# Hybrid decoder trunk: three adding transfers per up slab, and another order for forming slabs

## The chip, the cores and the metric

The kernel runs on one core of a Trainium2 chip (trn2). The metric is device time in microseconds (us), the median of repeated executions. Engines are named as in the profile: PE (TensorE, matrix products), ACT (ScalarE), DVE (VectorE), POOL (GpSimd), SP (SyncE, which here only issues DMAs). Each engine runs its own instructions in order; engines wait for one another by semaphores.

## The reference, cut to what matters

All of it is float32, with 16 meta tokens ahead of 512 tokens and a model width of 1024, in two layers:

```
u = rms_norm(h, norm_mix[l]);  proj = u @ w_in[l]          # conv branch, q, k, v, gates
...                                                        # depthwise conv, differential attention
h = h + merged @ w_o[l]
u = rms_norm(h, norm_mlp[l])
h = h + jnp.square(jax.nn.relu(u @ w_up[l])) @ w_down[l]   # w_up 1024 x 4096, w_down 4096 x 1024
```

The change touches only how the product `u @ w_up[l]` is fed.

## The kernel before

**Weights.** All weights come in slabs of 128 partitions x 2048 float32 (1 MB). There are two buffers of each kind, used in turn (`b = m % 2`): `w_raw` takes what SP loads, and a number is split into a high part (`w_hi`, rounded to fp32r) and a low part (`w_lo`, the rest). Each product of matrices is three matmuls: high by high, high by low, low by high.

**The MLP.** Per layer there are four groups g; each has four up slabs m = 0 to 3 and then four down slabs. An up slab is multiplied by a seven-product scheme on quarters of the matrix (`PRODUCTS`, in the order p1, p5, p2, p6, p7, p4, p3; 12 matmuls each). A slab has quarters A11, A21, A12, A22 of `QUAD` columns. Products p1, p5, p2 and p6 use the early forms (A11; the sum S1; A12; the sum S2), in `w_hi` and `w_lo`. Products p7, p4 and p3 use the late forms (S3, A22, S4), in `x_hi` and `x_lo`. Below, "slab 0 to 3" is an up slab m of a group.

**Who forms what.**
- DVE `sums_early(g, m)` (L1960, L1961) makes S1 and S2 from the landed slab; `sums_late(g, m)` (L1972, L1973) makes the two late sums, once `x_lo` of the slab before is finished.
- ACT `early_neg(g, m)` (L1224, L1225) writes the negated early forms from `w_raw` and `s2` into `w_lo`; `early_high` (L1230, L1231) writes the rounded ones into `w_hi`; `late_plain` (L1238) and `late_sums` (L1244) write `x_hi`.
- POOL `early_low(g, m)` issues two adding DMAs (L735 of 768 KB and L736 of 256 KB). These are written by the source as `w_lo += w_raw` and `w_lo += s2`, and both count on one semaphore `low_landed[b]`. They follow a small instruction `tick` (L734), which waits for `w_neg`.
- POOL `late_parts(g, m, parts)` (L747) computes `x_lo` in three parts of four instructions each: part 0 (plain, A22), part 1 (first late sum) and part 2 (second late sum).
- ACT `first_product` (L1252) copies p1's result out of PSUM, and `hidden_high(m, j)` (L1258 relu, L1259 square) handles one half of a finished slab. DVE `u2_sum`, `c22_sum`, `c21_sum`, `c12_sum` (L2008 to L2027) add up the seven products; `hidden_low` (L2038) and `square_up` (L2033) finish the hidden values.

**What sets the order.** The order on each engine is written out by hand in the loops over g and m. The waits that matter here are these:
- PE starts p1 of slab m when both transfers of its low part have landed, `early_high(m)` is done, and DVE has done `u2_sum(m - 1)`. PE starts p5 after `c22_sum(m - 1)`, p6 after `first_product(m)`, p7 after part 1 of `x_lo(m)`, and p3 after part 2.
- DVE `sums_early(3)` stands in the pass m = 1, between `c22_sum(1)` and `c21_sum(1)`.
- ACT `early_neg(3)` stands in the pass m = 1, ahead of `late_sums(2)` and `hidden_high(1, 1)`.
- POOL has, in every group, part 0 of `x_lo(2)`, then `early_low(3)`, then parts 1 and 2 of `x_lo(2)`, then all of `x_lo(3)`, then the low part of the first down slab (L634).
- SP loads the slab m + 2 (L604) when the low part of slab m has landed, among other waits.

Of the kernel before, what the change touches and what calls it, by code (L numbers as in the profile page):

```python
# [26 lines left out]
ALU = mybir.AluOpType  # L27
# [252 lines left out]
def build(nc, x_t, w_slabs, pvecs, rows_in, ident_in, mask_in, identb_in, out, h_spill, r_rows):  # L280
    ctx = ExitStack()
    with ctx:
# [161 lines left out]
        u_raw, t_raw, f_hi, f_ready = sem("u_raw"), sem("t_raw"), sem("f_hi"), sem("f_ready")  # L444
        sum_early, sum_late, sums_read = sem("sum_early"), sem("sum_late"), sem("sums_read")
        w_neg, w_form, w_late = sem("w_neg"), sem("w_form"), sem("w_late")
        low_landed, late_low = [sem("low_landed0"), sem("low_landed1")], sem("late_low")
        q_full, p1_done, u2_done, c22_done, tile_sum, relu_done = (sem(x) for x in ("q_full", "p1_done", "u2_done", "c22_done", "tile_sum", "relu_done"))
        v_chain, a_chain, p_chain = sem("v_chain"), sem("a_chain"), sem("p_chain")

# [28 lines left out]
        def a_read(layer, tile, k):  # L479

            return k + ((layer * A_TILES + tile) // 2 + 1)
# [88 lines left out]
        @block.sync  # L570
        def _(sp):
            slabs = w_slabs.rearrange("(i b) p c -> b i p c", b=2)
            for k, landed in enumerate(h_landed):
                if k in (1, 2):
                    half = slice((k - 1) * SLAB // 2, k * SLAB // 2)
                    sp.dma_start(w_raw[:, 0, half], slabs[0, 0, :, half]).then_inc(w_landed[0] if k == 2 else half_landed, 16)
                sp.dma_start(h[:, 2 * k:2 * k + 2, :], x_t[:, 2 * k:2 * k + 2, :]).then_inc(landed, 16)
            for dst, src in ((ident, ident_in), (maskb, mask_in), (identb, identb_in)):
                sp.dma_start(dst[:], src).then_inc(in_landed, 16)
            sp.dma_start(w_raw[:, 1, :], slabs[1, 0]).then_inc(w_landed[1], 16)  # L580

            def load_slabs(first, last):

                with sp.Fori(first // 2, last // 2) as i:
                    for b in range(2):
                        sp.wait_ge(w_ready, 2 * i + (b - 1))
                        sp.dma_start(w_raw[:, b, :], slabs[b, ds(i, 1)].rearrange("o p c -> p (o c)")).then_inc(w_landed[b], 16)

            start = 2
            for layer in range(LAYERS):  # L590
                load_slabs(start, up_slab(layer, 0, 2))
                for g in range(4):
                    for m in range(8):
                        s = up_slab(layer, g, m + 2)
                        if m < 4:
                            n = up_nth(layer, g, m)
                            sp.wait_ge(low_landed[n % 2], 32 * (n // 2 + 1))
                            sp.wait_ge(w_form, n + 1)
                            sp.wait_ge(late_low, 2 * n + 1)
                            sp.wait_ge(sum_late, n + 1)  # L600
                        else:
                            sp.wait_ge(w_ready, s - 1)
                        if s < LAYERS * SLABS:
                            sp.dma_start(w_raw[:, s % 2, :], slabs[s % 2, s // 2]).then_inc(w_landed[s % 2], 16)  # L604
                start = (layer + 1) * SLABS + 2
            for i in range(NT):

                sp.wait_ge(h_new, (LAYERS - 1) * NT + i + 1)
                sp.dma_start(out[:, i, :], h[:, i, META:T]).then_inc(stored, 16)
            sp.wait_ge(stored, 16 * NT)  # L610
# [3 lines left out]
        def _(pool):  # L614
# [73 lines left out]
            for layer in range(LAYERS):  # L688
# [39 lines left out]
                def early_low(g, m):  # L728

                    b, n = m % 2, up_nth(layer, g, m)  # L730
                    pool.wait_ge(w_neg, n + 1)
                    if n > 1:
                        pool.wait_ge(low_landed[b], 32 * (n // 2))
                    chain.link(nc.gpsimd.tensor_tensor(tick[:], ones[:, 0:1], ones[:, 0:1], ALU.mult))  # L734
                    pool.dma_start(w_lo[:, b, 0:3 * QUAD], w_raw[:, b, 0:3 * QUAD], accum_op=ALU.add).then_inc(low_landed[b], 16)  # L735
                    pool.dma_start(w_lo[:, b, 3 * QUAD:SLAB], s2[:, b, :], accum_op=ALU.add).then_inc(low_landed[b], 16)  # L736

                def late_parts(g, m, parts):

# [10 lines left out]
                plain, summed = (0,), (1, 2)  # L750
                early_low(0, 0)
                for g in range(4):
                    early_low(g, 1)
                    if g == 0:
                        late_parts(g, 0, plain + summed)
                        late_parts(g, 1, plain + summed)
                        early_low(g, 2)
                    else:
                        late_parts(g, 1, plain)
                        early_low(g, 2)  # L760
                        late_parts(g, 1, summed)
                    late_parts(g, 2, plain)
                    early_low(g, 3)
                    late_parts(g, 2, summed)
                    late_parts(g, 3, plain + summed)
                    for d in range(4):
                        down_low(g, d)
                    if g < 3:
                        early_low(g + 1, 0)
                        late_parts(g + 1, 0, plain + summed)  # L770
# [4 lines left out]
        def _(pe):  # L775
# [70 lines left out]
            def up_products(layer, g, m):  # L846
# [2 lines left out]
                n2 = span(layer)[1] // 2  # L849
                formed = layer * N_FORMS if (g, m) == (0, 0) else None  # L850
                tiles = (layer * A_TILES + A_MLP + 8 * g) // 2
                pe.wait_ge(low_landed[b], 32 * (n // 2 + 1))
                pe.wait_ge(w_form, n + 1)
                if n:
                    pe.wait_ge(u2_done, n)
                if formed is not None:
                    pe.wait_ge(f_ready, formed + 2 * KH)
                for k, (f, x, name) in enumerate(PRODUCTS):
                    if name == "p5" and n:
                        pe.wait_ge(c22_done, n)  # L860
                    if name == "p6":
                        pe.wait_ge(p1_done, n + 1)
                    elif name == "p2" and m < 2:
                        if (g, m) == (0, 1):
                            pe.wait_ge(sums_read, layer + 1)
                        pe.wait_ge(a_free[0], tiles)
                        pe.wait_ge(a_free[1], tiles)
                    elif name == "p2":
                        pe.wait_ge(hid_ready, 2 * (n - 1))
                    elif name == "p7":  # L870
                        if m:
                            pe.wait_ge(hid_ready, 2 * n - 1)
                        pe.wait_ge(late_low, 2 * n + 2)
                    elif name == "p3":
                        pe.wait_ge(w_ready, s + 1)
# [287 lines left out]
        def _(act):  # L1163
# [250 lines left out]
            for layer in range(LAYERS):  # L1414
# [91 lines left out]
                for i in range(NT):  # L1506
                    if i in (1, 3):
                        w_high_part(layer, s0 + 6 + i // 2)
                    if i == NT - 3:
                        early_neg(layer, 0, 0)  # L1510
                    if i == NT - 1:
                        early_neg(layer, 0, 1)
                    act.wait_ge(a_free[i % 2], a_read(layer, A_O, i // 2))
                    norm_raw(layer, i)
                    form_plain(layer, i)
                    if i == NT - 1:
                        late_plain(layer, 0, 0)
                    form_sum(layer, i)
                    if i == NT - 1:
                        first_product(layer, 0, 0)  # L1520
                        late_sums(layer, 0, 0)
                    if i >= KH:
                        form_last(layer, i)
                    norm_square(layer, i)
                    if i == NT - 2:
                        early_high(layer, 0, 0)
                    if i == NT - 1:
                        early_high(layer, 0, 1)
                for kk, (what, g) in enumerate(MLP_ORDER):
                    if what == "up":  # L1530
                        for m in range(4):
# [5 lines left out]
                                first_product(layer, g, m)  # L1537
                            if m == 1 and g == 0:
                                late_sums(layer, g, 1)
                            if m:  # L1540
                                hidden_high(layer, g, m - 1, 0)
                            if m == 1 and g == 0:
                                early_neg(layer, g, 2)
                            if m < 3:
                                late_plain(layer, g, m + 1)
                            if m < 3 and (m or g):
                                early_high(layer, g, m + 1)
                            if m == 1 or m == 0 and g:
                                early_neg(layer, g, m + 2)
                            if m < 3 and (m or g):  # L1550
                                late_sums(layer, g, m + 1)
                            hidden_high(layer, g, m, 1)
# [26 lines left out]
        def _(dve):  # L1579
# [176 lines left out]
            for layer in range(LAYERS):  # L1756
# [291 lines left out]
                for kk, (what, g) in enumerate(MLP_ORDER):  # L2048
                    if what == "up":
                        for m in range(4):  # L2050
                            if m:
# [3 lines left out]
                                    announce(dve, V.tensor_scalar(halves(r_inv2, layer), mlp_sum(layer)[1], 1.0 / D, NORM_EPS, ALU.mult, ALU.add), sums_read, layer + 1)  # L2055
                                hidden_low(g, m - 1, 1)
                                square_up(g, m - 1, 0)
                            if m == 1 and g == 0:
                                sums_early(g, 2)
                            if m < 3 and (m or g):  # L2060
                                sums_late(g, m + 1)
                            if m:
# [8 lines left out]
                            square_up(g, m, 1)  # L2071
                            if m == 0 and g == 0:
                                sums_late(g, 1)
                        c12_sum(g, 3)
                        hidden_low(g, 3, 1)
                        square_up(g, 3, 0)
# [100 lines left out]
```

## Time and profile before

| | |
|---|---|
| device time, 3 runs | median 1875.01 us (1873.65 to 1876.04) |
| profiled execution | 1878.18 us, of which the span is 1876.4 us |
| busy share of the span | PE 96%, PEld 88%, DVE 70%, POOL 63%, ACT 44% |
| chain that ended last | PE 69%, POOL 10%, DVE 7%, DMA 5%, ACT 4%, issue 4% |
| up slabs (matmuls of L883) | 578 to 632 us and 678 to 907 us in layer 0, 1502 to 1556 us and 1601 to 1827 us in layer 1, with down slabs between |

The profile is that of one execution. Busy time of PE is the time in which matmuls were in flight. The chain is followed back from the last instruction to what released each wait, so it names the work that set the end. A wait's releaser is the one whose signal came last.

### The profile page before, as it was taken

The numbers are of one execution on the slowest core, as the hardware profiler recorded it, in microseconds if no ns is written. First come the engines' busy times: TensorE is split into PE (matmuls) and PEld (weight loads), VectorE is DVE, ScalarE is ACT, GpSimd is POOL, SyncE is SP. The second block draws the span as 40 slices with busy tenths as digits, with TensorE's granted clock in tenths as the row PEclk, the third lists the DMA queues.
The fourth block names the chain that finished last, engine by engine and source line by source line (L and its number), as shares of the span: only waits on it lengthen the run. The fifth ranks groups of instructions, "written<-read, shape, count | busy, mean of one in ns | idle before, by whom it ended". The sixth has DMA issues, their size and how long they took to land.

```text
span 1876.4 us, 34787 instructions
## 1 busy us (share of the span) xinstructions
PE 1806.8 (96%) x13053; PEld 1650.9 (88%) x13053; DVE 1311.5 (70%) x2085; ACT 823.4 (44%) x1745; POOL 1173.1 (63%) x2240
## 2 busy tenths in 40 slices
PE   9999999999997999999999999999999989999989
PEld 8999888889997999999999998887678788888787
DVE  7998888777456555646569989888865664647462
ACT  4135565436246343535421355553453563525260
POOL 4777445546774666666687664446477566676664
PEclk9999999999998999999999999999999989999999
DMA  4222111112325463637432221111233362736362
GB/s 176 90 91 68 30 62 46 64 50 92 137 90 137 132 159 113 166 104 173 135 113 90 88 71 46 46 49 65 67 108 126 106 151 99 178 107 164 116 159 85
DMA packets 34794, 194.54 MB, mean 104 GB/s; under 512 B 4048, under 2 KB 4432, under 8 KB 16992
## 3 DMA queue, kind: packets, MB, share of 16 engines
q1 hardware_dynamic: 21888, 147.01, 22.9%
q0 software_dynamic: 9216, 33.56, 9.6%
q10 hardware_dynamic: 3552, 12.15, 1.8%
q8 instruction: 84, 1.38, 0.3%
q14 instruction: 54, 0.44, 0.1%
HBM read 154.85 MB, written 4.29 MB: 85 GB/s over the span
## 4 chain that ended last, share of the span: by engine, by line
PE 69%; POOL 10%; DVE 7%; DMA 5%; ACT 4%; issue 4%; DVEq 0%; POOLq 0%; ACTq 0%
PE psum L789 40%; PE psum L928 13%; PE psum L883 4%; POOL w_lo L634 3%; DMA w_lo<-s 3%; POOL w_lo L627 3%; PE psum L1025 2%; PE psum L993 2%; DMA w_raw<-w_slabs 2%; PE psum L942 2%; POOL x_lo L747 2%; PE psum L1013 1%; ACT e L1343 1%; DVE h L2103 1%; PE psum L1070 1%
## 5 line engine op out<-in xcount | busy, mean ns | idle before, releaser
L634 POOL TENSOR_TENSOR w_lo<-w_raw,w_hi 128x128 fp32r<-128x128 f32 x1152 | 560.6, 525 | 222.5 <-ACT w_hi L1325 194.3
L789 PE MATMUL psum<-u,w_hi 128*128 128x264 f32 (+1 forms) x2112 | 407.7, 308 | 9.1 <-POOL w_lo L627 5.0
L789 PEld LDWEIGHTS psum<-u,w_hi 128*128 128x128 f32 x2112 | 310.0, 189 | 31.5 <-POOL w_lo L627 6.5
L789 PE MATMUL psum<-hid,w_hi 128*128 128x264 f32 (+1 forms) x1536 | 328.3, 322 | 5.7 <-POOL w_lo L634 5.7
L560 DVE SCALAR_TENSOR_TENSOR psum<-xg,pvec,psum 128x512 f32<-128x512 f32 x440 | 301.0, 750 | 4.6 <-DVE xg L1815 2.2
L928 PE MATMUL psum<-w_hi,u 128*128 128x256 f32 x1536 | 287.7, 287 | 0.1
L789 PEld LDWEIGHTS psum<-hid,w_hi 128*128 128x128 f32 x1536 | 237.3, 188 | 30.3 <-issue 7.0
L789 PE MATMUL psum<-u,w_lo 128*128 128x264 f32 (+1 forms) x1056 | 251.2, 304 | 0.0
L928 PEld LDWEIGHTS psum<-w_hi,u 128*128 128x128 f32 x1536 | 237.6, 189 | 10.7 <-issue 10.3
L627 POOL TENSOR_TENSOR w_lo<-w_raw,w_hi 128x128 fp32r<-128x128 f32 x480 | 237.4, 532 | 2.5
L928 PE MATMUL psum<-w_lo,u 128*128 128x256 f32 x768 | 215.9, 281 | 0.0
L1325 ACT CAST w_hi<-w_raw 128x2048 fp32r<-128x2048 f32 x72 | 137.4, 1908 | 173.8 <-PE psum L789 173.8
L789 PE MATMUL psum<-hid,w_lo 128*128 128x264 f32 (+1 forms) x768 | 204.8, 321 | 0.0
L883 PE MATMUL psum<-uh,w_hi 128*128 128x264 f32 (+1 forms) x512 | 152.6, 298 | 36.6 <-DMA w_lo<-s 15.8
L789 PEld LDWEIGHTS psum<-u,w_lo 128*128 128x128 f32 x1056 | 170.6, 189 | 8.5
L2102 DVE TENSOR_TENSOR down_tmp<-psum,r_inv 128x512 f32<-128x512 f32 (+1 forms) x56 | 39.1, 699 | 165.9 <-PE psum L789 165.7
L883 PE MATMUL psum<-ul,w_hi 128*128 128x264 f32 (+1 forms) x512 | 148.4, 290 | 0.0
L883 PE MATMUL psum<-uh,w_lo 128*128 128x264 f32 (+1 forms) x512 | 148.1, 289 | 0.0
L928 PEld LDWEIGHTS psum<-w_lo,u 128*128 128x128 f32 x768 | 145.4, 189 | 0.0
L747 POOL TENSOR_TENSOR x_lo<-s,x_hi 128x128 fp32r<-128x128 f32 x256 | 127.7, 906 | 22.7 <-ACT x_hi L1244 22.7
L883 PEld LDWEIGHTS psum<-uh,w_hi 128*128 128x128 f32 x512 | 100.4, 196 | 42.6 <-DMA w_lo<-s 17.8
L789 PEld LDWEIGHTS psum<-hid,w_lo 128*128 128x128 f32 x768 | 127.7, 188 | 11.2
(253 smaller groups left out, 3606.6 us busy)
## 6 DMA issues: line engine op xcount, KB each, us to landing
w_raw<-w_slabs SPq DMA_DIRECT2D x135, 1024.0 KB, 4.9
w_lo<-w_raw POOLq DMA_DIRECT2D x32, 768.0 KB, 5.9
w_lo<-s POOLq DMA_DIRECT2D x32, 256.0 KB, 6.8
h<-x_t SPq DMA_DIRECT2D x4, 528.0 KB, 7.3
h<-x_t ACTq DMA_DIRECT2D x1, 2112.0 KB, 9.5
h_spill<-h ACTq DMA_DIRECT2D x8, 264.0 KB, 2.7
h<-h_spill ACTq DMA_DIRECT2D x1, 2112.0 KB, 8.4
out<-h SPq DMA_DIRECT2D x8, 256.0 KB, 2.2
```

Source lines behind the costliest of these rows:

```text
L560: return nc.vector.scalar_tensor_tensor(out=done if ends else acc, in0=x, scalar=w, in1=done if begins else acc, op0=ALU.mult, op1=ALU.add)
L627: last = nc.gpsimd.tensor_tensor(w_lo[:, b, c:c + P], w_raw[:, b, c:c + P], w_hi[:, b, c:c + P], ALU.subtract)
L634: last = nc.gpsimd.tensor_tensor(w_lo[:, b, c:c + P], w_raw[:, b, c:c + P], w_hi[:, b, c:c + P], ALU.subtract)
L747: last = nc.gpsimd.tensor_tensor(x_lo[:, b, cut], source[:, c:c + P], x_hi[:, b, cut], ALU.subtract)
L789: last = nc.tensor.matmul(psum[:, 2 * slot + j, 0:n], w[:, b, cut], src[:, part, kc, at0:at0 + n], start=(kc == 0 and m == 0), stop=(kc == ...
L883: last = nc.tensor.matmul(quad(layer, m, name), w[:, cut], act_[:, x, kc, 0:n2], start=(kc == 0 and j == 0), stop=(kc == KH - 1 and j == 2))
L928: done = nc.tensor.matmul(psum[0:tn, B_BANK[n], 0:2 * P], u[:, part, kc, t0:t0 + tn], w[:, b, kc * 2 * P:(kc + 1) * 2 * P], start=k == 0, ...
L942: last = nc.tensor.matmul(psum[0:2 * META, bank, 0:2 * P], meta_u[:, kc, :], w[:, b, kc * 2 * P:(kc + 1) * 2 * P], start=kc == 0 and w is ...
L993: nc.tensor.matmul(psum[0:tn, banks[c], at0:at0 + k1 - k0], qk[rows64, 0, hh % 2, qp, t0:t0 + tn], qk[rows64, 1, hh % 2, kp, k0:k1], start ...
L1025: last = nc.tensor.matmul(psum[:, bank, (i - 1) * P:SEQ], v_sb[0:kn, hh // 2 % 2, j, cut], a_t[0:kn, b0:b0 + n, :].rearrange("p a b -> p ( ...
L1325: nc.scalar.copy(w_hi[:, b, :], w_raw[:, b, :]).then_inc(w_high, 1)
L2102: announce(dve, V.tensor_tensor(row(down_tmp[:], layer), a_ps(layer, j), row(r_inv2[:], layer), ALU.mult), a_free[j], a_read(layer, A_MLP ...
```

## The change

It does four things.

1. The low part of an up slab comes by three adding DMAs of 256, 512 and 256 KB in place of two of 768 and 256 KB. Each has its own semaphore. PE waits for the first ahead of p1, for the second ahead of p5 and for the third ahead of p6. SP and POOL wait for all three.
2. In the first group of each layer, slab 2 is formed earlier on DVE and ACT: `sums_early(0, 2)` moves to the end of the pass m = 0, and `early_neg(0, 2)` goes ahead of `hidden_high(0, 0)`. On POOL, part 0 of `x_lo(0)` goes ahead of `early_low(1)`, and `early_low(2)` goes ahead of part 2 of `x_lo(1)`.
3. In the last step of the output projection, `late_plain(0, 0)` goes to the front and `early_neg(0, 1)` behind the last `form_sum`.
4. In all eight groups `early_neg(3)` moves on ACT from the pass m = 1 to the pass m = 2, behind `first_product(2)`.

```diff
-        low_landed, late_low = [sem("low_landed0"), sem("low_landed1")], sem("late_low")
+        low_landed, late_low = [[sem(f"low_landed{b}{part}") for part in "abc"] for b in range(2)], sem("late_low")
...
-                    pool.dma_start(w_lo[:, b, 0:3 * QUAD], w_raw[:, b, 0:3 * QUAD], accum_op=ALU.add).then_inc(low_landed[b], 16)
-                    pool.dma_start(w_lo[:, b, 3 * QUAD:SLAB], s2[:, b, :], accum_op=ALU.add).then_inc(low_landed[b], 16)
+                    pool.dma_start(w_lo[:, b, 0:QUAD], w_raw[:, b, 0:QUAD], accum_op=ALU.add).then_inc(low_landed[b][0], 16)
+                    pool.dma_start(w_lo[:, b, QUAD:3 * QUAD], w_raw[:, b, QUAD:3 * QUAD], accum_op=ALU.add).then_inc(low_landed[b][1], 16)
+                    pool.dma_start(w_lo[:, b, 3 * QUAD:SLAB], s2[:, b, :], accum_op=ALU.add).then_inc(low_landed[b][2], 16)
...
                 for g in range(4):
+                    if g == 0:
+                        late_parts(g, 0, plain)
                     early_low(g, 1)
                     if g == 0:
-                        late_parts(g, 0, plain + summed)
-                        late_parts(g, 1, plain + summed)
+                        late_parts(g, 0, summed)
+                        late_parts(g, 1, plain + summed[0:1])
                         early_low(g, 2)
+                        late_parts(g, 1, summed[1:2])
...
-                pe.wait_ge(low_landed[b], 32 * (n // 2 + 1))
+                pe.wait_ge(low_landed[b][0], 16 * (n // 2 + 1))
...
-                    if name == "p5" and n:
-                        pe.wait_ge(c22_done, n)
+                    if name == "p5":
+                        pe.wait_ge(low_landed[b][1], 16 * (n // 2 + 1))
+                        if n:
+                            pe.wait_ge(c22_done, n)
                     if name == "p6":
+                        pe.wait_ge(low_landed[b][2], 16 * (n // 2 + 1))
                         pe.wait_ge(p1_done, n + 1)
...
                     if i == NT - 3:
                         early_neg(layer, 0, 0)
+                    act.wait_ge(a_free[i % 2], a_read(layer, A_O, i // 2))
+                    if i == NT - 1:
+                        late_plain(layer, 0, 0)
+                    norm_raw(layer, i)
+                    form_plain(layer, i)
+                    form_sum(layer, i)
                     if i == NT - 1:
                         early_neg(layer, 0, 1)
-                    act.wait_ge(a_free[i % 2], a_read(layer, A_O, i // 2))
-                    norm_raw(layer, i)
-                    form_plain(layer, i)
-                    if i == NT - 1:
-                        late_plain(layer, 0, 0)
-                    form_sum(layer, i)
...
                             if m == 1 and g == 0:
                                 late_sums(layer, g, 1)
+                                early_neg(layer, g, 2)
+                            if m == 2:
+                                early_neg(layer, g, 3)
                             if m:
                                 hidden_high(layer, g, m - 1, 0)
-                            if m == 1 and g == 0:
-                                early_neg(layer, g, 2)
                             if m < 3:
                                 late_plain(layer, g, m + 1)
                             if m < 3 and (m or g):
                                 early_high(layer, g, m + 1)
-                            if m == 1 or m == 0 and g:
-                                early_neg(layer, g, m + 2)
+                            if m == 0 and g:
+                                early_neg(layer, g, 2)
...
-                            if m == 1 and g == 0:
-                                sums_early(g, 2)
                             if m < 3 and (m or g):
                                 sums_late(g, m + 1)
...
                             square_up(g, m, 1)
                             if m == 0 and g == 0:
                                 sums_late(g, 1)
+                                sums_early(g, 2)
```

## Rows read from the trace of the kernel before

**Rows 1.** Waits of PE, whole span: us in total, times, longest us.
```profile
PE psum L883 <- DMA w_lo<-s: 15.8, 8, 5.5
```

**Rows 2.** Chain that ended last, layer 0 group 1: start us, us, what.
```profile
682.34 7.82 DMA w_lo<-s
...
690.20 7.60 PE psum L883 x60
...
698.76 0.70 DVE w_raw L1960
...
700.22 1.49 ACT w_lo L1224
...
702.79 0.87 POOL w_lo L735
...
704.56 3.39 POOL x_lo L747 x8
...
723.83 0.36 PE psum L789
```

**Rows 3.** The chain in other groups, same columns: layer 0 groups 2, 3; layer 1.
```profile
781.44 8.68 DMA w_raw<-w_slabs
...
873.55 3.38 POOL x_lo L747 x8
...
1792.31 10.19 DMA w_raw<-w_slabs
```

**Rows 4.** The chain in the first group of layer 0 and of layer 1.
```profile
608.67 22.96 PE psum L883 x168
...
1533.15 22.72 PE psum L883 x168
```

**Rows 5.** Timeline of ACT, layer 0 group 1: start us, us, engine, line.
```profile
703.06 0.60 ACT L1258 ACTIVATE relu<-psum 128x528 f32<-128x528 f32 x1
703.70 0.65 ACT L1259 ACTIVATE hid<-relu 128x528 fp32r<-128x528 f32 x1
704.25 0.36 ACT L1252 COPY r_inv<-psum 128x264 f32<-128x264 f32 x1
```

**Rows 6.** Timelines of DVE and of POOL, layer 0 group 1.
```profile
700.22 0.44 DVE L2022 TENSOR_TENSOR psum<-psum,q_u 128x264 f32<-128x264 f32 x1
...
703.38 1.19 POOL L736 DMA_DIRECT2D w_lo<-s  x1
703.94 4.00 POOL L747 TENSOR_TENSOR x_lo<-s,x_hi 128x128 fp32r<-128x128 f32 x8
```

**Rows 7.** Timeline of PE, layer 0 group 1: the first matmul of slab 2's p7.
```profile
706.43 0.36 PE L883 MATMUL psum<-uh,x_hi 128*128 128x264 f32 x1
```

**Rows 8.** SP's load of slab 3, layer 0 group 1; its time to landing (last).
```profile
690.17 0.33 SPq L604 DMA_DIRECT2D w_raw<-w_slabs  x1
...
w_raw<-w_slabs SPq DMA_DIRECT2D x1, 1024.0 KB, 7.6
```

**Rows 9.** Timelines of POOL and of DVE in the first group of layer 0.
```profile
595.96 4.36 POOL L747 TENSOR_TENSOR x_lo<-s,x_hi 128x128 fp32r<-128x128 f32 x8 [5.20 <-ACT x_hi L1244]
...
600.42 0.69 DVE L1972 TENSOR_TENSOR s<-w_raw,s 128x512 f32<-128x512 f32 x1 [1.69 <-POOL x_lo L747]
...
604.33 0.76 DVE L1960 TENSOR_TENSOR w_raw<-w_raw 128x512 f32<-128x512 f32 x1
```

**Rows 10.** Stretch in the first group: busy us (instructions) by engine, then PEclk.
```profile
607.00:614.00 7.00, 5.33 (x25) 5.33 (x26) 2.81 (x5) 5.31 (x10) 5.45 (x12) 0.51 0.79 178
```

**Rows 11.** The page's DMA queue (MB, share of 16 engines) and DMA issues (landing).
```profile
q0 software_dynamic: 9216, 33.56, 9.6%
...
w_lo<-w_raw POOLq DMA_DIRECT2D x32, 768.0 KB, 5.9
w_lo<-s POOLq DMA_DIRECT2D x32, 256.0 KB, 6.8
...
out<-h SPq DMA_DIRECT2D x8, 256.0 KB, 2.2
```

More of the change, by code:

```diff
@@ L596, in _ @@
                             n = up_nth(layer, g, m)
-                            sp.wait_ge(low_landed[n % 2], 32 * (n // 2 + 1))
+                            for landed in low_landed[n % 2]:
+                                sp.wait_ge(landed, 16 * (n // 2 + 1))
                             sp.wait_ge(w_form, n + 1)
@@ L732, in early_low @@
                     if n > 1:
-                        pool.wait_ge(low_landed[b], 32 * (n // 2))
+                        for landed in low_landed[b]:
+                            pool.wait_ge(landed, 16 * (n // 2))
                     chain.link(nc.gpsimd.tensor_tensor(tick[:], ones[:, 0:1], ones[:, 0:1], ALU.mult))
-                    pool.dma_start(w_lo[:, b, 0:3 * QUAD], w_raw[:, b, 0:3 * QUAD], accum_op=ALU.add).then_inc(low_landed[b], 16)
-                    pool.dma_start(w_lo[:, b, 3 * QUAD:SLAB], s2[:, b, :], accum_op=ALU.add).then_inc(low_landed[b], 16)
+                    pool.dma_start(w_lo[:, b, 0:QUAD], w_raw[:, b, 0:QUAD], accum_op=ALU.add).then_inc(low_landed[b][0], 16)
+                    pool.dma_start(w_lo[:, b, QUAD:3 * QUAD], w_raw[:, b, QUAD:3 * QUAD], accum_op=ALU.add).then_inc(low_landed[b][1], 16)
+                    pool.dma_start(w_lo[:, b, 3 * QUAD:SLAB], s2[:, b, :], accum_op=ALU.add).then_inc(low_landed[b][2], 16)
                 def late_parts(g, m, parts):
```

## The prediction

> **What bounds the kernel now.** I read the shares first: PE is busy for 96% of the span and holds 69% of the chain that ended last. So nearly everything is paced by PE, and only a wait of PE, or a chain that goes round PE through a group, can move the end. Second, I read PE's waits. The largest releaser is the low part of an up slab, 15.8 us in 8 waits [rows 1]. The change is aimed at these. Two of them are the first groups' slab 2, 5.4 and 5.5 us; the other six share 4.9 us.
>
> Third, I read the chain that ended last, in order of time, because a wait that goes is worth only what the next bound leaves. In layer 0's group 1 [rows 2] it runs: landing of slab 1's low part, PE to 697.8, DVE `sums_early(3)` at 698.76, ACT `early_neg(3)` at 700.22, POOL's DMAs at 702.79, `x_lo(2)` parts 1 and 2 at 704.56, then DVE, ACT and POOL until the first down slab starts at 723.83. So from `sums_early(3)` on, the group's end is not set by PE. It is set by one chain through `early_neg(3)` and `early_low(3)`, since POOL computes parts 1 and 2 of `x_lo(2)` only behind `early_low(3)`. In other groups the chain doesn't even enter by PE's wait: in layer 0's group 2 and layer 1's group 3 it goes from slab 1's low part through SP's load of slab 3 (8.68 and 10.19 us) to `sums_early(3)` [rows 3]. Layer 1's groups 1 and 2 look the same; layer 0's group 3 enters by `x_lo(1)` on POOL.
>
> **The six later groups.** Removed: the wait of p1(1) for the full low part, 4.9 us in all [rows 1]. The first 256 KB should be down about 3.3 us after issue. That is worked out from the queue's rate, 33.56 MB in 9.6% of 1876 us, or 186 GB/s, so 1.4 us for 256 KB and 4.2 us for 768 KB. The 768 KB landed in 5.9 us, which leaves 1.7 us around the data [rows 11]. That wait then ends before PE arrives, and the second and third parts have 1.45 and 4.4 us more (one and three products of 12 matmuls).
>
> Added on the chain, per group:
> - `early_neg(3)` stood directly behind `sums_early(3)`. Now `hidden_high(1, 1)` and `first_product(2)` go ahead of it on ACT, and `hidden_high(1, 1)` waits for `c21_sum(1)`, which stands behind `sums_early(3)` on DVE. That is 0.44 us for L2022 [rows 6], and relu, square and copy, from 703.06 to 704.61, 1.5 us [rows 5]: 1.9 us.
> - A third DMA ahead of `x_lo(2)` part 1. Two issues start 0.59 us apart and the next instruction 0.56 us later [rows 2, 6]: 0.6 us.
> - Sum 2.5 us. `early_neg(3)` also waits for slab 2's p1 to be finished, which is earlier than this in every group.
>
> This delay has no cover. Part 1 of `x_lo(2)` ended at half of its 4.00 us, 705.9 [rows 6], and p7(2) began at 706.43 [rows 7]. So PE will reach p7(2) and stand there 2 to 4 us. Behind it nothing in the group has slack, as rows 2 show up to 723.83.
>
> What comes off depends on how early `sums_early(3)` can start:
> - Layer 0, group 1: PE is 1.5 us earlier, but slab 3 lands at 690.17 + 7.6 = 697.8 [rows 8], against the start at 698.76. So 0.9 us comes off: +1.6.
> - The four groups bound by the load: the load still waits for all of the low part, whose bytes haven't changed. Nothing comes off, or up to 0.9 us if slab 3's packets get through sooner between smaller low ones. I take 0.3 off, nearer to none, as no row shows such a gain: 4 x 2.2 = +8.8.
> - Layer 0, group 3: `x_lo(1)` stands behind `early_low(2)` [rows 3] and gets a third DMA too: 2.5 + 0.6 = +3.1.
>
> Together +13.5 us, with bounds of +9 (0.9 off in all six, no extra DMA) and +16.
>
> **The first groups.** The 5.4 us before p1(2) is mostly removed: `sums_early(2)` needs no wait for `square_up(0, 0)` any more. But look at what ends later. A third DMA ahead of `x_lo(0)` part 1 makes PE 0.6 late. `x_lo(1)` parts 1 and 2 took 4.36 us from 595.96 [rows 9], 2.2 us each. Now part 1 ends at 598.7. Then `early_low(2)` takes 0.5 for the tick and its gap, and 3 x 0.57, and part 2 ends at 603.1, where it was 600.3. DVE's `sums_late(2)` waits for that. It began at 600.42 and DVE then ran without a pause to `sums_early(3)` at 604.33 [rows 9], so that now starts at 607.1 and ends at 608.7. The 1.9 us of before puts `early_neg(3)` at 610.6. In rows 2 it is 2.57 us from there to the first DMA, 613.2; then 1.7 for three DMAs and 2 x 2.1 for the parts, 619.1. In group 1, part 2 ended at 707.95 and the down slab started at 723.83, 15.9 us later [rows 2]: 635.0. Before, it started at 608.67 + 22.96 = 631.6 [rows 4]. So +3.4, and I take +3.3 for each layer, as layer 1's stretch has nearly the same length (22.72). Bounds: 0, if the chain behind part 2 shrinks by what PE gained, and +5.
>
> That contains the clock. After the 5.4 us pause the granted clock was 0.51 for a stretch of 7 us, the 1.2 GHz level [rows 10], which cost PE about 2.5 us. In the new order PE's pause moves to p7(2), about 4 to 5 us long, and may drop the clock again; I count no gain.
>
> The reordering at the end of the output projection hides behind PE's first three products. `sums_late(0, 1)` and then `sums_early(0, 2)` now run ahead of L2055, which p2(1) waits for: about 1 us of PE, absorbed by the later chain. The added semaphore waits of PE and SP cost nothing that I can see: products with and without a wait that is already met start 1.45 us apart. At most 0.02 us each, 64 of them, 1.3 us.
>
> **A rule of the skill.** The two transfers of a slab are overlapped: issued 0.59 us apart, they landed 5.9 and 6.8 us after issue, so 1.5 us apart, which is the data time of 256 KB [rows 6, 11]. The Trainium skill (DMA: Bandwidth & Descriptors, Anatomy of one DMA — SWDGE (gpsimd) path) gives each such DMA about 2.0 us of fixed cost beside its bytes, and advises large transfers. If that were paid one after another, a third transfer would put the full landing 2 us back; the row says it is overlapped.
>
> **The sum.** 13.5 + 2 x 3.3 = 20.1 us. Of the profiled execution this makes 1878.2 + 20.1 = 1898.3 us. That execution took 1878.18 us, 3.2 above the median of the runs, so against the median the forecast is 1895 us.
>
> **The rivals.**
> - *Partly relieved chain.* Slab 3 lands sooner, and the later stations lose waits among themselves (DVE's L1972 stretched beside POOL, say). The six groups give +6 and the first groups +2 together: 1883. For it: L0 group 1 has 0.9 us of this kind. Against: three entries of the chain through a load. Chance 0.15.
> - *Faster.* The chain through `early_low(3)` doesn't bind, since POOL gets `x_lo(2)` part 1 done in time for p7(2). Then the 4.9 us go, and each first group gains 4 us of wait and 2.5 us of clock: 4.9 + 13 = 18, less 3 for DMAs and DVE: 1860. The point from which it decides: part 1 would have to end by 704.9 in group 1 (p7(2) less the 1.5 us gained), where 705.9 was its end before anything was put ahead of it. Chance 0.07.
> - *No change.* The new wait at p7(2) costs only what the wait at p1(1) gave, about 0.8 us a group, and the first groups end as before: 1875. Chance 0.04.
> - *More clock drops.* The six new pauses of 2 to 4 us each bring a stretch at 1.2 GHz, at some 1 us beyond the slack: 1901. Chance 0.03.
> - *Transfers in series.* A lone transfer of 256 KB, on another queue, took 2.2 us to land [rows 11]. If the third one adds this to the full landing, the load of slab 3 is 2.2 us later in four groups: 1895 + 9 = 1904. Chance 0.03.
>
> My forecast has 0.68. Its own range is 1888 to 1900. The range with the partly relieved chain is 1882 to 1901; it leaves out the faster case, no change and the series. Within 0.2% (3.7 us), about what a measurement of this kernel can tell from no change, lies only the no-change case. Faster 0.07, same 0.04, slower 0.89.
>
> **What would show it.** PE's wait for `w_lo` before p1(1) gone in all six groups. A new wait of PE before p7(2) on `x_lo` L747, 2 to 5 us, in all eight. `early_neg(3)` behind L1252. p1(2) of the first groups at about 604 to 606, not 608.67. The first down slab's start later by about 2.5 us per group. If p7(2) doesn't wait, or the down slabs start no later, the prediction is wrong at its root. If p7(2) waits but the groups end less than 1 us later, the tail of 15.9 us was mis-sized.

## The result, and the profile after

The changed kernel takes 1901.41 us (median of 4 runs, 1900.81 to 1902.34), against 1874.33 us for the kernel before on the same chip: ratio 1.0143, interval 1.0127 to 1.0159. So it is slower, as forecast, but by 27.1 us where 20.1 had been summed; 1901.4 lies 0.4 us above the range.

The profiled execution took 1900.81 us, 22.6 more than the profiled one of before. The first rows of the page and of its queues and issues, as in [rows 11]:

```profile
PE 1812.1 (95%) x13053; PEld 1658.1 (87%) x13053; DVE 1305.1 (69%) x2085; ACT 824.8 (43%) x1745; POOL 1212.5 (64%) x2272
...
q0 software_dynamic: 13824, 33.56, 9.9%
...
w_lo<-w_raw POOLq DMA_DIRECT2D x32, 512.0 KB, 5.6
w_lo<-w_raw POOLq DMA_DIRECT2D x32, 256.0 KB, 3.6
w_lo<-s POOLq DMA_DIRECT2D x32, 256.0 KB, 6.5
```

The first part of a low slab lands in 3.6 us, where the prediction had 3.3, and the wait of [rows 1] is gone. Another has taken its place. PE's waits over the whole span (us in total, times, longest):

```profile
PE psum L892 <- POOL x_lo L750: 42.6, 10, 5.2
```

PE's timeline at p1(2) of the first group and at p7(2) of group 1, layer 0, which answer to [rows 4, 7] (start us, us, what; idle time before it in brackets):

```profile
607.26 0.36 PE L892 MATMUL psum<-uh,w_hi 128*128 128x264 f32 x1 [1.56 <-DVE r_inv L2018]
...
714.36 0.56 PE L892 MATMUL psum<-uh,x_hi 128*128 128x264 f32 x1 [4.97 <-POOL x_lo L750]
```

Eight of the ten waits are those ahead of p7(2), 4.97 to 5.18 us, one in each group. The chain that ended last, layer 0 group 1, against [rows 2]:

```profile
688.21 6.44 DMA w_lo<-s
...
694.77 9.03 DMA w_raw<-w_slabs
...
703.88 0.70 DVE w_raw L1970
704.61 0.70 DVE s L1971
705.34 0.45 DVE psum L2032
705.81 0.62 ACT relu L1267
...
707.01 0.36 ACT r_inv L1261
707.37 1.39 ACT w_lo L1233
708.75 0.53 ACT w_lo L1234
...
709.84 0.88 POOL w_lo L737
710.72 0.90 POOL w_lo L738
711.61 0.89 POOL w_lo L739
712.50 3.35 POOL x_lo L750 x8
...
731.34 3.66 PE psum L795 x28
```

Two things stand here. First, between `sums_early(3)` and `early_neg(3)` there are now `c21_sum(1)`, relu and copy. ACT's timeline has the start of `early_neg(3)` at 707.27, so this is 3.4 us from 703.88, where it was 1.46. Second, the chain now enters this group too by the third transfer and SP's load, which it did not in [rows 2].

From p1(0) to the first down slab the groups were 45.48, 44.63, 45.31 (layer 0) and 45.79, 45.18, 46.24 us (layer 1), and are 48.32, 49.14, 49.45 and 48.69, 48.13, 48.32: +19.4 us for the six. The first groups went from 53.05 and 54.00 to 56.72 and 56.27: +5.9. Together that is +25.4 us (these, and all means over groups below, are worked out from the first matmul of each group and slab in the traces).

### The profile page after: what moved, and what is told of

Same layout as the page of the kernel before. It is cut to its first block, busy times and chain, and to the rows that moved or that the text cites. A ratio compares the mean times of both kernels' runs of the same rounds, so it can differ in the third digit from the quotient of the medians.

```text
span 1899.0 us, 34940 instructions
## 1 busy us (share of the span) xinstructions
PE 1812.1 (95%) x13053; PEld 1658.1 (87%) x13053; DVE 1305.1 (69%) x2085; ACT 824.8 (43%) x1745; POOL 1212.5 (64%) x2272
## 3 DMA queue, kind: packets, MB, share of 16 engines
q0 software_dynamic: 13824, 33.56, 9.9%
HBM read 154.85 MB, written 4.29 MB: 84 GB/s over the span
## 4 chain that ended last, share of the span: by engine, by line
PE 66%; POOL 11%; DVE 8%; ACT 5%; issue 5%; DMA 5%; DVEq 0%; POOLq 0%; ACTq 0%; SPq 0%
PE psum L795 39%; PE psum L937 13%; POOL w_lo L635 3%; POOL w_lo L628 3%; PE psum L892 2%; DMA w_raw<-w_slabs 2%; PE psum L1002 2%; PE psum L1034 2%; DMA w_lo<-s 2%; POOL x_lo L750 2%; PE psum L951 2%; PE psum L1022 1%; ACT w_lo L1233 1%; POOL w_lo L737 1%; DVE h L2112 1%
## 5 line engine op out<-in xcount | busy, mean ns | idle before, releaser
L892 PE MATMUL psum<-uh,w_hi 128*128 128x264 f32 (+1 forms) x512 | 149.2, 291 | 15.5 <-issue 8.8
L892 PE MATMUL psum<-uh,x_hi 128*128 128x264 f32 (+1 forms) x384 | 117.2, 305 | 42.8 <-POOL x_lo L750 42.6
L750 POOL TENSOR_TENSOR x_lo<-s,x_hi 128x128 fp32r<-128x128 f32 x256 | 136.9, 1162 | 17.1 <-ACT x_hi L1253 17.1
L892 PE MATMUL psum<-ul,w_hi 128*128 128x264 f32 (+1 forms) x512 | 146.7, 287 | 0.0
L892 PE MATMUL psum<-uh,w_lo 128*128 128x264 f32 (+1 forms) x512 | 146.6, 286 | 0.0
```

Of the source, the lines that this page charges most:

```text
L750: last = nc.gpsimd.tensor_tensor(x_lo[:, b, cut], source[:, c:c + P], x_hi[:, b, cut], ALU.subtract)
L892: last = nc.tensor.matmul(quad(layer, m, name), w[:, cut], act_[:, x, kc, 0:n2], start=(kc == 0 and j == 0), stop=(kc == KH - 1 and j == 2))
```

## The experiments

Each was timed beside the kernel before, whose median there was 1874.9 to 1876.1 us. "Split" is the low part in three transfers.

| | kernel | us | ratio (interval) |
|---|---|---|---|
| 1 | changed, `early_neg(3)` back | 1886.6 | 1.0054 (1.0036 to 1.0072) |
| 2 | before + split | 1885.2 | 1.0046 (1.0031 to 1.0060) |
| 3 | changed + POOL's `x_lo(2)` first | 1854.5 | 0.9890 (0.9863 to 0.9916) |
| 4 | before + `early_neg(3)` moved | 1896.0 | 1.0101 (1.0081 to 1.0120) |
| 5 | 2 + earlier load | 1879.9 | 1.0027 (1.0017 to 1.0036) |
| 6 | 3 + earlier load | 1850.1 | 0.9862 (0.9845 to 0.9879) |
| 7 | 3 without the split | 1875.6 | 1.0003 (0.9987 to 1.0019) |
| 8 | 4 + POOL's `x_lo(2)` first | 1876.2 | 1.0003 (0.9991 to 1.0015) |
| 9 | changed without the split | 1891.2 | 1.0086 (1.0069 to 1.0103) |
| 10 | before + POOL's `x_lo(2)` first | 1892.6 | 1.0094 (1.0078 to 1.0111) |
| 11 | 6, `early_neg(3)` back | 1865.9 | 0.9953 (0.9937 to 0.9970) |
| 12 | before + one `tick` more per low slab | 1888.4 | 1.0072 (1.0055 to 1.0089) |

**1. `early_neg(3)` back in the pass m = 1.**

```diff
-                            if m == 2:
-                                early_neg(layer, g, 3)
...
-                            if m == 0 and g:
-                                early_neg(layer, g, 2)
+                            if m == 1 or m == 0 and g:
+                                early_neg(layer, g, m + 2)
```

> The changed kernel with one part undone: early_neg(3) is back in the pass m = 1, ahead of late_sums(2), in all eight groups; three transfers and the first groups' order stay. Theory A (the loss is the chain early_neg(3), early_low(3), x_lo(2), and the move of early_neg(3) puts 1.9 us on it in every group, 8 x 1.9 = 15 of the 27 us): 1883 to 1888, and PE's wait before p7(2) on x_lo falls from about 5 us to 0 to 3 us a group. Rival B (the loss is the three transfers, with their later full landing and a third issue on POOL): the time stays at 1895 or more.

By the medians 14.8 us of the 27 came back, by the ratios 16.7, where 8 x 1.9 is 15. The step from `sums_early(3)` to `early_neg(3)` was 1.45 us again in all eight groups, against 3.34 to 3.38.

**2. The split alone, in the kernel before.** The edit is part 1 of the change.

> The kernel before with three transfers and their waits alone, no order changed. Theory A: POOL's third issue (0.6 us) and the later full landing put about 1.3 us on each of the six later groups, +8, and the first groups' slab 2 starts about 3 us sooner, of which 1 to 2 us stay, -3: 1878 to 1882. Rival B: most of the 27 us is here, 1890 or more. Rival C (PE's wait before p1 was worth something): under 1871.

Neither: +9 us, between what the two theories gave. The step from the start of `early_neg(3)` to part 1 of `x_lo(2)` went from 3.72 to 4.25 us, the forecast 0.5. But `sums_early(3)` also came later, by 5.7 us in the six later groups together. That is not in my sum.

**3. POOL does parts 1 and 2 of `x_lo(2)` ahead of `early_low(3)`,** in the changed kernel.

```diff
                     late_parts(g, 2, plain)
-                    early_low(g, 3)
                     late_parts(g, 2, summed)
+                    early_low(g, 3)
```

> The changed kernel with one thing more: on POOL, parts 1 and 2 of x_lo(2) go ahead of early_low(3) in all groups, so that they no longer wait for early_neg(3). Theory A: PE's wait before p7(2) goes, slab 3's first transfer still lands in time for p1(3), and a group becomes shorter than in the kernel before, by about 2.5 us, since its chain no longer runs through the load of slab 3: 1855 to 1862. Rival B (three transfers): still above 1880. Rival D (early_low(3) gets late, and PE's wait moves to p1(3)): 1875 to 1895.

1854.5 us: 47 less than the changed kernel and 21 less than the kernel before. POOL's timeline in layer 0's group 1 (start us, us, engine, line):

```profile
694.20 3.85 POOL L750 TENSOR_TENSOR x_lo<-s,x_hi 128x128 fp32r<-128x128 f32 x8 [0.45 <-ACT x_hi L1253]
702.64 0.20 POOL L736 TENSOR_TENSOR tick<-ones 128x1 f32<-128x1 f32 x1 [4.59 <-ACT w_lo L1234]
703.14 0.87 POOL L737 DMA_DIRECT2D w_lo<-w_raw  x1 [0.30 <-POOL tick L736]
```

The two parts start when `x_hi` is there, 8.4 us ahead of the tick that they stood behind. PE's waits at L892 for `x_lo` fell from 42.6 to 1.7 us, and the largest for data there is now for the low part. Nearly all of it, 0.8 to 1.1 us in each group, is ahead of p5(3), which needs slab 3's second transfer:

```profile
PE psum L892 <- DMA w_lo<-w_raw: 8.6, 10, 1.1
```

**4. `early_neg(3)` moved, alone, in the kernel before** (the reverse of the edit of experiment 1).

> The kernel before with early_neg(3) moved alone, behind first_product(2) in the pass m = 2. Two transfers. Theory A: +1.9 us in each of eight groups, 1888 to 1891, and a wait of PE before p7(2) of 2 to 3.5 us. Rival B (three transfers): within 3 us of 1875.

+20 us. The later groups give 12.1, as forecast for this step (6 x 1.95 = 11.7). The first groups give 6.8: there it started 7.6 us behind `sums_early(3)` and not 1.7, since `first_product(2)` stands ahead of it and p1(2) was still late (part 2 of the change isn't in). So parts 2 and 4 of the change aren't independent.

**5. The split, and SP's load behind two parts only.**

```diff
-                            for landed in low_landed[n % 2]:
+                            for landed in low_landed[n % 2][:2]:
                                 sp.wait_ge(landed, 16 * (n // 2 + 1))
...
+                    if up_nth(layer, g, m) > 1:
+                        dve.wait_ge(low_landed[b][2], 16 * (up_nth(layer, g, m) // 2))
```

> The kernel before with the three transfers and their waits only (as the second experiment, 1.0046 of before, which is 1882.7 us at 1874), and SP's load of slab n+2 waits for only the first two parts of the low part of slab n; DVE's sums_early, which writes the third part's source, waits for the third. Theory H1, the extra microsecond per group is the later full landing that holds SP's load of slab 3: the load is issued about 1 us earlier in the four groups bound by it, sums_early(3) starts some 1 us earlier, and the time falls by 4 to 6 us, to 1877 to 1879. Theory H2, the load isn't late because of its wait but because its packets share the queue with more small ones: the load is issued earlier and lands no earlier, 1882 to 1886.

1879.9, near the first theory: 4 us by the ratios, 5 by the medians. The intervals of 2 and 5 overlap by a little, so the traces have to decide. The load of slab 3 was issued 1.46 us earlier on average, and `sums_early(3)` of the six groups came 4.1 us earlier in all. In layer 1's group 1 it did not: the load was issued 1.34 us earlier and landed no earlier.

**6. The same edit in experiment 3's kernel.**

> The changed kernel with parts 1 and 2 of x_lo(2) ahead of early_low(3) on POOL (as the third experiment, 1854.5 us), and SP's load of slab n+2 waits for only the first two parts. In that order the chain to the end of a group no longer goes through slab 3's load. If that is so, nothing changes: 1852 to 1857. If the load is what now ends the group, the time falls by 4 us or more, to 1850 or less.

1850.1 us, the best time of any version here. Against experiment 3 it is between the two expectations and the intervals overlap (0.9845 to 0.9879, 0.9863 to 0.9916), so the gain of this edit in that order isn't shown.

**7. Experiment 3 without the split** (part 1 of the change taken out).

> The third experiment's kernel (parts 1 and 2 of x_lo(2) ahead of early_low(3)) with two transfers and one signal per slab as before: what the three transfers are worth in the order where the chain through early_low(3) is gone. If their worth is the wait of p1(1), p1(2) and p1(3) for the full low part: low(3) is issued 4 us later in this order, so p1(3) waits for a full landing that is some 3 to 4 us after the first part's; six to eight groups times 3 us or more, 1870 to 1885. If PE's waits for the low part are covered there too: 1852 to 1858.

The gain is gone: 1875.6 us. Its waits of PE:

```profile
PE psum L886 <- DMA w_lo<-s: 28.1, 17, 3.7
```

With `early_low(3)` behind the parts of `x_lo(2)`, p1(3) needs slab 3's low part soon after its issue. In experiment 3, with a signal for each transfer, PE waited at p1(3) only once, 0.55 us, and 0.8 to 1.1 us ahead of p5(3). Here it waits 1.8 to 3.7 us ahead of p1(3) in every group. So the split is worth 21 us in this order and costs 9 in the old one.

**8. `early_neg(3)` moved and POOL's `x_lo(2)` first, no split, no part 2.** The edits of 4 and 3.

> The kernel before with two of the moves alone: early_neg(3) behind first_product(2) on ACT, and parts 1 and 2 of x_lo(2) ahead of early_low(3) on POOL; two transfers, the first groups' slab 2 as before. If POOL's order is the key and early_neg(3)'s place then costs nothing: the p7(2) waits are gone and the group's chain is shorter by early_low(3)'s 1.8 us or more, but p1(3) waits for a low part issued 4 us later: 1865 to 1880. If the low part of slab 3 comes too late for PE without its first part's own signal: over 1880.

1876.2 us, as the first of the two expectations had it. The moved `early_neg(3)`, which costs 20 us alone, costs nothing once POOL's order follows it.

**9. The changed kernel without the split.**

> The changed kernel with two transfers and one signal per slab as before: both reorderings without the split of the low part. If the cost of the change is a sum of parts, the split's share is the 0.46% that it cost alone: about 1892 (1889 to 1896), with sums_early(3) of the six later groups 5 us earlier in all than in the changed kernel. If the split already pays a part back here, because the pauses of PE for the full low part return: 1898 or more.

1891.2, as a sum of parts has it: without the split the time is 10 us less and `sums_early(3)` comes 4.8 us earlier in the six groups. Against experiment 4 it also shows what part 2 of the change (with part 3) does: its first groups take 110.6 us together, those of experiment 4 113.9 (from the traces; the ratios don't tell the two apart).

**10. POOL's `x_lo(2)` first, alone, in the kernel before.**

> The kernel before with one move alone: parts 1 and 2 of x_lo(2) ahead of early_low(3) on POOL. It leaves early_neg(3) where it was, so slab 3's low part can be issued as soon as POOL is through with x_lo(2). If PE's wait for that low part is what holds the group in this order (32 us of waits in the eighth experiment), and its issue is set by POOL alone, the time is as in the eighth experiment, 1874 to 1878. If early_neg(3) sets the issue, it comes up to 1.9 us a group earlier: 1862 to 1870. If slower than before by over 0.2%, POOL's order is no gain without the split at all.

Slower by 18 us: the last of the three cases expected, which had no mechanism. ACT and POOL in layer 0's group 1 (timelines), then the waits of PE over the span:

```profile
701.21 1.49 ACT L1224 ACTIVATE w_lo<-w_raw 128x1536 fp32r<-128x1536 f32 x1 [4.27 <-DVE s L1961]
702.61 0.61 ACT L1225 ACTIVATE w_lo<-s 128x512 fp32r<-128x512 f32 x1
703.12 1.03 ACT L1244 CAST x_hi<-s 128x1024 fp32r<-128x1024 f32 x1
```

```profile
704.24 3.40 POOL L747 TENSOR_TENSOR x_lo<-s,x_hi 128x128 fp32r<-128x128 f32 x8 [6.86 <-ACT x_hi L1244]
707.61 0.18 POOL L734 TENSOR_TENSOR tick<-ones 128x1 f32<-128x1 f32 x1
```

```profile
PE psum L883 <- DMA w_lo<-s: 39.0, 15, 5.5
```

I had missed that ACT is in order too: `late_sums(2)` (L1244), which writes the `x_hi` that POOL subtracts, stands behind `early_neg(3)` (L1224). So POOL stood idle for 6.86 us, and the transfers left only behind both. In experiment 8 the same parts began at 697.33, 17.7 us after p1(0) instead of 24.5:

```profile
697.33 4.29 POOL L747 TENSOR_TENSOR x_lo<-s,x_hi 128x128 fp32r<-128x128 f32 x8 [0.60 <-ACT x_hi L1244]
```

**11. Experiment 6 with `early_neg(3)` back.**

> The sixth experiment's kernel (POOL's parts of x_lo(2) first, load of slab n+2 behind two parts only; 0.9862 of before) with early_neg(3) back directly behind sums_early(3). If PE's waits for the first part of slab 3's low part (7.8 us in 11 waits there) still hold the groups and early_neg(3) sets its issue: 4 to 8 us less, 1842 to 1847. If POOL sets it: 1848 to 1852.

+16 us instead of a gain, for the same reason: part 1 of `x_lo(2)` starts 5.9 us later in layer 0's group 2, and PE's waits at L892 for `first_product` (L1261) went from 1.3 to 14.2 us. With experiments 8 and 10 this shows that POOL's new order needs the move on ACT for its full worth. It isn't worthless without it, once there is the split: 1865.9 is 20.7 us below experiment 1, of which the earlier load may be 4 to 5 (experiment 5). Without the split POOL's order alone cost 18.

**12. The time of a third issue without its packets.**

```diff
+                    chain.link(nc.gpsimd.tensor_tensor(tick[:], ones[:, 0:1], ones[:, 0:1], ALU.mult))
                     pool.dma_start(w_lo[:, b, 3 * QUAD:SLAB], s2[:, b, :], accum_op=ALU.add).then_inc(low_landed[b], 16)
```

> The kernel before, two transfers with one signal, and between their two issues one more tiny instruction on POOL (128x1, 0.19 us, with its gap some 0.5 us), about what issuing a third transfer takes; no byte and no packet is added. Theory ISSUE, the split delays slab 3 because it takes POOL's time ahead of x_lo and ahead of the last transfer's issue: the full landing of slab 1's low part and sums_early(3) come later as in the second experiment (about 5 us in six groups together, of which 3 or more should show), x_lo(2) part 1 starts 0.5 us further behind early_neg(3), and PE keeps its waits at p1(1): 1884 to 1892. Theory PACKETS, it is the larger number of small packets: sums_early(3) moves by under 1 us in six groups together, and only the 0.5 us behind early_neg(3) are added: 1878 to 1882.

POOL in layer 0's group 2; with the tick between, the issues are 0.8 to 0.9 us further apart (1.3 in layer 0's group 3), more than the 0.5 that I meant to add:

```profile
775.25 0.89 POOL L735 DMA_DIRECT2D w_lo<-w_raw  x1 [0.30 <-POOL tick L734]
775.86 0.51 POOL L736 TENSOR_TENSOR tick<-ones 128x1 f32<-128x1 f32 x1
776.67 0.88 POOL L737 DMA_DIRECT2D w_lo<-s  x1 [0.30 <-POOL tick L736]
```

1888.4 us in the median (the profiled execution was the fastest of four, 1882.3), and `sums_early(3)` later by 4.3 us in the six groups: POOL's time alone delays the load. It isn't all of it. Mean of the six groups, us:

| | before | 12 | 2 | changed |
|---|---|---|---|---|
| p1(0) to first issue of slab 1's low part | 3.65 | 4.27 | 4.29 | 4.00 |
| from there to its full landing | 7.37 | 7.39 | 7.98 | 7.81 |
| SP's load of slab 3 issued | 11.04 | 11.68 | 12.40 | 11.94 |

In experiment 2 half of the delay is the later issue and half is a longer time in the queue, which experiment 12 with its unchanged packets doesn't have. Experiment 12 shows one thing more: its last transfer is issued 0.9 us further behind the first, and the full landing comes no later for it (7.39 us against 7.37). So a later last issue doesn't by itself explain the longer time in the queue.

## Why the prediction was wrong, point by point

**The term that failed** is what comes off ahead of `sums_early(3)`: "the load still waits for all of the low part, whose bytes haven't changed. Nothing comes off, or up to 0.9 us". I took 0.9 + 4 x 0.3 = 2.1 off, and 0.6 on in layer 0's group 3, so -1.5 us in the six groups. Measured: +0.46, +2.13, +1.30, +0.51, +0.61, -0.25, together +4.8. These 6.3 us make the difference between the 13.5 us predicted for the six groups and the 19.4 measured (the third DMA ahead of `x_lo(2)` was 0.4 us less than summed, in all six together). The chain that the prediction followed stood; this size in it was off, and had the wrong sign. Nor did the upper bound of +16 allow for it, as it let nothing come on ahead of `sums_early(3)`.

Its cause can be read in layer 0's group 2, where the chain goes the same way in both traces. The chain in the kernel before (start us, us, what):

```profile
765.74 3.58 DVE h L2103
...
774.07 0.57 POOL w_lo L735
...
774.65 6.77 DMA w_lo<-s
```

The chain in the changed kernel:

```profile
773.26 4.08 DVE h L2112
...
782.21 0.88 POOL w_lo L737
...
783.34 6.71 DMA w_lo<-s
...
790.17 9.59 DMA w_raw<-w_slabs
...
799.85 0.70 DVE w_raw L1970
```

PE's timeline, p1(0) of this group, in the kernel before and in the changed one:

```profile
770.64 0.28 PE L883 MATMUL psum<-uh,w_hi 128*128 128x264 f32 x1
```

```profile
778.15 0.28 PE L892 MATMUL psum<-uh,w_hi 128*128 128x264 f32 x1
```

Counted from p1(0):
- The third issue of slab 0's low part puts off `x_lo(0)` on POOL. DVE's addition of the last down slab runs beside these subtractions and ends only with them (last section), so it takes 4.08 us instead of 3.58. `sums_early(1)` and `early_neg(1)` come behind it.
- So slab 1's low part has its first issue at 4.06 instead of 3.43, and the last of its three transfers is issued at 5.19, where the last of two was at 4.01.
- It lands at 11.90 instead of 10.78, and SP's load follows: 9.59 us against 8.68 [rows 3]. `sums_early(3)` starts at 21.70 instead of 19.57.

I had charged the third issue once per group, ahead of `x_lo(2)`. Slab 0's comes in front of the load as well. Experiment 12 shows this by POOL's time alone (first issue 0.62 us later, `sums_early(3)` 4.3 us later in the six groups), experiment 2 shows the whole by the split alone (+5.7 us), experiment 5 by letting the load go earlier (4.1 us back). One group shows the reverse: in layer 1's group 1 of the changed kernel DVE's addition was not held (0.78 us), and slab 1's first issue came at 2.86 us instead of 3.87. Of the longer time in the queue, 0.4 to 0.6 us, I can say only that it comes with the split: the queue has 13824 packets where it had 9216 for the same 33.56 MB.

The load isn't the last wait in all six groups. In layer 1's groups 1 and 2 of the changed kernel slab 3 had landed 3.9 and 1.3 us before `sums_early(3)`. There DVE's `sums_late(2)` (L1982) waits for `x_lo(1)`, which stands on POOL behind slab 2's three issues, the path that the prediction had seen for layer 0's group 3 alone. DVE's timeline, layer 1, group 1:

```profile
1631.96 1.28 DVE L1982 TENSOR_TENSOR s<-w_raw,s 128x512 f32<-128x512 f32 x1 [2.68 <-POOL x_lo L750]
```

Two numbers of the working were wrong in themselves. The lower bound of +9 for the six groups doesn't follow from its own words: 0.9 us off in all six and no extra DMA leaves 6 x 1.0 = 6. And 1.7 + 1.4 us makes 3.1 for the first 256 KB, not 3.3; 3.6 was measured. Neither decides the result.

**Right, and of the right size.**
- ACT's order: 1.9 us predicted, 1.89 to 1.93 measured in the six later groups; experiment 1 gave 14.8 us back.
- The third DMA ahead of `x_lo(2)`: 0.6 predicted, 0.54 measured.
- All eight waits at p7(2) came, 4.97 to 5.18 us, at the top of the 2 to 5 forecast and just above it.
- Behind `x_lo(2)` there was no slack: from p7(2) to the first down slab the later groups take 17.0 us on average, before 17.3.
- The first groups: +5.9 us against 6.6. p1(2) started at 607.26, beyond the 604 to 606 forecast, though not because of the low part: it waits for `u2_sum(1)` (L2018), which stands on DVE behind `sums_late(2)`, and that waited for `x_lo(1)` until 604.03:

```profile
604.03 1.27 DVE L1982 TENSOR_TENSOR s<-w_raw,s 128x512 f32<-128x512 f32 x1 [3.82 <-POOL x_lo L750]
```

- Layer 0's group 1 was to have +1.6 and had +2.84: its 0.9 us of relief didn't come, for the reason above.

All together, the groups give 25.4 us. The medians differ by 27.1 and the profiled executions by 22.6. Between the MLPs of the two layers, where the change does nothing, the trace of before takes 3.5 us more, with two stretches of 3.4 us at half clock at 1200.9 and 1395.5 us that the changed one doesn't have; and the changed one is 1.1 us late at its first p1(0). Without these the profiled executions differ by 25.0 us. So it is luck that the changed one's 1900.8 us lies so near the 1898.3 forecast for it. The 1.7 us from 25.4 to the difference of the medians stay unexplained.

**The rivals.**
- *More clock drops* foresaw something true. Behind each p7(2) pause the granted clock falls to the 1.2 GHz level. Windows of the first two groups (busy us by engine, then PEclk, DMA share, GB/s):

```profile
619.00:622.40 3.40, 3.16 (x15) 3.19 (x16) 1.56 (x2) 0.00 (x0) 3.40 (x9) 0.54 0.87 159
714.30:717.70 3.40, 3.34 (x15) 3.37 (x16) 1.75 (x2) 0.00 (x0) 3.40 (x8) 0.50 0.74 135
```

  All eight groups have one, 3.4 or 6.8 us long. But it wasn't the cause of the missing 6 us. The stretch in which it falls, p7(2) to the down slab, got no longer in the six later groups (17.3 us before, 17.0 now), since DVE, ACT and POOL set its end.
- *Transfers in series* came out near the time (1904) by the wrong price. The time from first issue to full landing grew by 0.44 us (0.61 in experiment 2), not by 2.2. The Trainium skill (DMA: Bandwidth & Descriptors, Anatomy of one DMA — SWDGE (gpsimd) path) gives each such transfer about 2.0 us beside its bytes; the trace agrees with the prediction's reading that this isn't paid one after another.
- *Faster* fell, but its condition was the right one to ask about. The source of `x_lo(2)` was ready. ACT in layer 0's group 1:

```profile
699.86 1.05 ACT L1253 CAST x_hi<-s 128x1024 fp32r<-128x1024 f32 x1 [1.00 <-DVE s L1983]
705.81 0.61 ACT L1267 ACTIVATE relu<-psum 128x528 f32<-128x528 f32 x1 [4.90 <-DVE psum L2032]
```

  `x_hi` is done at 700.9 and POOL starts on it at 712.50, because `early_low(3)` stands ahead and waits for `early_neg(3)`. Counted from p1(0), it is done after 17.9 us, where it was 24.8 (703.2) before. So the move on ACT is half of a pair. It frees `x_lo(2)` from `early_neg(3)` on ACT, and POOL's order still ties the two together, by a longer path than before. With POOL's order turned as well, and the split, the time is 1854.5 us, and 1850.1 with the earlier load.

## What to carry to other kernels

When an instruction is moved back on one in-order engine, look at every engine that waits for it and move what stands behind those waits: the same move cost 20 us or nothing, depending on POOL's order. An extra issue on a busy engine is to be charged at every place where that engine is on a path to the bound: here ahead of `x_lo(0)`, ahead of `x_lo(2)` and, in some groups, ahead of `x_lo(1)`, not once. And a split transfer pays only where its consumer is close behind the issue: here -21 us in one order and +9 in another.

## What wasn't expected of the hardware

A DVE addition of 128x528 from two tensors in SBUF took 0.71 us alone, and 3.58 and 4.08 us (in the chains of layer 0's group 2 above) while POOL ran its subtractions of `x_lo(0)` from SBUF. The one of 0.71 us, in the kernel before, DVE's timeline, 6 us later:

```profile
771.68 0.71 DVE L2103 TENSOR_TENSOR h<-h,down_tmp 128x528 f32<-128x528 f32 x1
```

The Trainium skill (SBUF — State Buffer, Who interferes with whom) says that such a DVE instruction and a POOL instruction that reads SBUF exclude each other, and that the second to start waits for the first. The slowing agrees, but the wait was not for one instruction. The row of `x_lo(0)` is twelve subtractions, with starts 0.42 us apart, and the addition lost 2.9 to 3.4 us. In the fourteen traces here, for the six later groups of each, the addition ended 1.1 to 1.3 us after the last subtraction of the row had started in 82 of 84 cases, however much of the row was left when it began. In the other two (layer 1's group 1, in the changed kernel and in experiment 3) it took 0.78 us, and three of POOL's starts were 0.86 to 0.98 us apart instead. So the addition was mostly held for the whole row; what made these two go the other way, no run here shows.

A tiny POOL instruction between two DMAs, 0.19 us where it stands behind idle time, cost 0.8 to 0.9 us in five of the six later groups (experiment 12). Left open is how much of the queue's longer time in the split comes from its packets and how much from what runs beside it.
